# Grouped attention on one core: two heads' queries turned together, keys in both partition halves, scores of two heads in a row

## What is computed

```
A_HEADS = 8; A_KV_HEADS = 2; A_HEAD_DIM = 64
qa_l = apply_rope(qa_l, cos, sin)
ka_l = apply_rope(ka_l, cos, sin)
o_a = attend_blocks(qa_l, jnp.concatenate([ka_c, ka_l], axis=1), jnp.concatenate([va_c, va_l], axis=1))
# attend_blocks, for each block of 128 queries and each head h with keys of head h // 4:
#   p = softmax(q @ k.T * 64 ** -0.5);  o = p @ v
```

## Time and profile before

| | us |
|---|---|
| median of 3 runs | 1925.68 |
| lowest and highest | 1921.84, 1927.43 |
| the profiled execution | 1927.77 |
| its span from first to last instruction | 1925.9 |

### The profile page before, as it was taken

One profiled execution on the slowest core, in us unless ns is written; L12 is line 12 of the kernel. 1 busy time (PEld: TensorE's weight loads), 2 busy tenths in 40 slices (PEclk: granted clock), 3 DMA queues, 4 the chain that ended last, 5 costly groups with the idle time before them and its releaser, 6 DMA issues.

```text
span 1925.9 us, 22240 instructions
## 1 busy us (share of the span) xinstructions
PE 1629.5 (85%) x9130; PEld 1050.3 (55%) x9130; DVE 635.8 (33%) x1474; ACT 407.7 (21%) x725; POOL 41.5 (2%) x58
## 2 busy tenths in 40 slices
PE   6999999989999999998797776777787976776776
PEld 4544567878888886556543433433355542442433
DVE  3277453138898445548300000000023100000001
ACT  4221331011220113212321211111123211111211
POOL 0000000001210000001000000000000000000000
PEclk8999999999999989889798988888897998888888
DMA  9536740273749824103999999999986999999996
GB/s 366 180 111 221 284 156 1 88 284 132 261 150 375 316 80 175 44 1 138 427 414 430 428 428 429 428 428 428 417 338 246 430 428 429 428 428 428 428 428 259
DMA packets 110831, 572.56 MB, mean 297 GB/s; under 512 B 9188, under 2 KB 15460, under 8 KB 86184
## 3 DMA queue, kind: packets, MB, share of 16 engines
q1 hardware_dynamic: 109776, 569.79, 73.3%
q10 hardware_dynamic: 984, 1.79, 0.3%
HBM read 570.51 MB, written 1.05 MB: 297 GB/s over the span
## 4 chain that ended last, share of the span: by engine, by line
PE 60%; DMA 31%; DVE 4%; ACT 2%; issue 1%; SPq 1%; DVEq 0%; ACTq 0%
DMA ring<-in_w_exp_up_dram 30%; PE bank L483 19%; PE bank L1213 10%; PE bank L886 8%; PE bank L913 4%; PE bank L491 2%; PE bank L1239 2%; PE bank L929 2%; PE bank L1249 2%; PE bank L1289 1%; PE bank L570 1%; PE bank L1200 1%; DMA ring<-in_w_ada_dram 1%; PE bank L580 1%; PE bank L625 1%
## 5 line engine op out<-in xcount | busy, mean ns | idle before, releaser
L1213 PE MATMUL bank<-ring,arena 128*32 128x512 f32 x1792 | 267.8, 753 | 195.4 <-DMA ring<-in_w_exp_up_dram 193.4
L1213 PEld LDWEIGHTS bank<-ring,arena 128*32 128x32 f32 x1792 | 70.7, 134 | 389.8 <-issue 354.2
L2556 DVE COPY arena<-bank 128x256 f32<-128x256 f32 x32 | 13.6, 424 | 606.4 <-PE bank L1229 606.4
L886 PE MATMUL bank<-hT,ring 128*128 128x256 f32 x704 | 155.6, 383 | 4.2 <-ACT hT L1447 4.2
L483 PE MATMUL bank<-ring,hT 128*128 128x512 f32 (+3 forms) x416 | 148.5, 513 | 1.6 <-DVE arena L2343 1.5
L886 PEld LDWEIGHTS bank<-hT,ring 128*128 128x128 f32 x704 | 134.9, 192 | 23.1 <-issue 4.6
L1780 ACT COPY arena<-bank 128x512 f32<-128x512 f32 x32 | 33.4, 1044 | 440.6 <-PE bank L1213 440.6
L1239 PE MATMUL bank<-ring,arena 128*32 128x512 f32 x960 | 125.1, 666 | 1.7 <-DVE arena L2560 1.7
L1249 PE MATMUL bank<-arena 128*128 128x256 f32 x512 | 118.8, 385 | 1.8 <-DVE arena L2568 1.8
L1852 DVE SCALAR_TENSOR_TENSOR spare<-ring,spare 128x512 f32<-128x512 f32 x154 | 116.3, 755 | 4.4
L1249 PEld LDWEIGHTS bank<-arena 128*128 128x128 f32 x512 | 94.6, 190 | 39.7 <-issue 28.1
(11 more groups left out here) (358 smaller groups left out, 1702.8 us busy)
## 6 DMA issues: line engine op xcount, KB each, us to landing
ring<-in_w_exp_down_dram SPq DMA_DIRECT2D x60, 2048.0 KB, 19.1
ring<-in_w_exp_gate_dram SPq DMA_DIRECT2D x56, 2048.0 KB, 19.0
ring<-in_w_exp_up_dram SPq DMA_DIRECT2D x56, 2048.0 KB, 23.3
ring<-in_w_mod_dram SPq DMA_DIRECT2D x24, 2048.0 KB, 12.4
ring<-in_w_ada_dram SPq DMA_DIRECT2D x12, 2048.0 KB, 13.9
ring<-in_w_up_dram SPq DMA_DIRECT2D x10, 2048.0 KB, 11.2
ring<-in_w_in_dram SPq DMA_DIRECT2D x8, 2048.0 KB, 14.3
arena<-in_w_exp_up_dram SPq DMA_DIRECT2D x6, 2048.0 KB, 24.2
```

What stands on the lines that cost most here:

```text
L886: ins = pe.matmul(b[:, 0:T], x[:, k, j * 128:j * 128 + 128], hT[:, k, 0:T], start=(k == 0), stop=(k == KD - 1))
L1213: ins = pe.matmul(bank[0][32 * q:32 * q + 32, :], xe[:, k * CAP:(k + 1) * CAP], xs[q // 2][:, o:o + 512], start=(k == 0), stop=(k == KD - ...
```

## The change

Keys and queries are laid out anew. The keys of each key-value head are turned twice, once into partitions 0 to 63 and once into 64 to 127, by plain matmuls against the identity (16 matmuls of 64 by 128). The queries of two heads are turned together, 128 channels at a time (8 turns). Each engine now copies two banks of 128 partitions, where it copied three of 64. The order of the steps becomes pair of heads, block, head (`head_block`), so that two steps next to each other are the two heads of a pair: one reads partitions 0 to 63 of `e_qT` and `e_kT`, the other 64 to 127. PE issues the scores two at a time, at even i. The output of a pair of heads takes its bank from the first ring. The latent attention (`mla`) keeps its order.

```
+def head_block(tag, i):
+    pair, r = divmod(i, 4)
+    return (pair, r % 2, r // 2) if tag == "gqa" else (pair, r // 2, r % 2)
...
-        e_qT = ar(4096, A_H, T)
+        e_qT = ar(4096, A_H // 2, T)
...
                 def scores(i):
                     b = G.open(pe, (tag, "s", i), second=True)
-                    h, qb = i // 2, i % 2
+                    hp, h2, qb = head_block(tag, i)
+                    h = 2 * hp + h2
...
                 def output(hp):
-                    b = G.open(pe, (tag, "o", hp), second=True)
+                    b = G.open(pe, (tag, "o", hp), second=tag == "mla")
...
                 for i in range(2 * heads):
-                    if i + 2 < 2 * heads:
+                    if tag == "gqa" and i % 2 == 0 and i + 2 < 2 * heads:
+                        scores(i + 2)
+                        scores(i + 3)
+                    if tag == "mla" and i + 2 < 2 * heads:
                         scores(i + 2)
...
             for g in range(A_KV):
                 b = G.open(pe, ("ekT", g))
-                turn(("ekT", g), b, [e_kv[:, tb, g * A_D:g * A_D + A_D] for tb in range(4)])
+                for tb in range(4):
+                    for lo in (0, A_D):
+                        ins = pe.matmul(b[lo:lo + A_D, tb * 128:tb * 128 + 128], e_kv[:, tb, g * A_D:g * A_D + A_D],
+                                        ident, start=True, stop=True, skip_group_check=True)
+                G.close(ins, ("ekT", g))
             pe.wait_ge(sem("heads_ready"), 3)
-            for hp in range(4):
-                b = G.open(pe, ("eqT", hp))
-                turn(("eqT", hp), b, [e_qa[:, tb, h * A_D:h * A_D + A_D] for h in (2 * hp, 2 * hp + 1) for tb in range(TB)])
+            for half in range(2):
+                b = G.open(pe, ("eqT", half))
+                turn(("eqT", half), b, [e_qa[:, tb, hp * 128:hp * 128 + 128] for hp in (2 * half, 2 * half + 1)
+                                        for tb in range(TB)])
...
-            attend("gqa", A_H, lambda h: e_qT[0:A_D, h, :], lambda h: e_kT[0:A_D, h // 4, :],
+            attend("gqa", A_H, lambda h: e_qT[A_D * (h % 2):A_D * (h % 2) + A_D, h // 2, :],
+                   lambda h: e_kT[A_D * (h % 2):A_D * (h % 2) + A_D, h // 4, :],
...
-            G.give(act.copy(e_kT[0:A_D, 1, :], G.take(act, ("ekT", 1))[0:A_D, :]), ("ekT", 1))
-            for hp in (1, 3):
-                G.give(act.copy(e_qT[0:A_D, 2 * hp:2 * hp + 2, :].rearrange("p a b -> p (a b)"),
-                                G.take(act, ("eqT", hp))[0:A_D, :]), ("eqT", hp))
+            evict(("ekT", 1), e_kT[:, 1, :])
+            evict(("eqT", 1), e_qT[:, 2:4, :].rearrange("p a b -> p (a b)"))
...
-            G.give(dve.tensor_copy(e_kT[0:A_D, 0, :], G.take(dve, ("ekT", 0))[0:A_D, :]), ("ekT", 0))
-            for hp in (0, 2):
-                G.give(dve.tensor_copy(e_qT[0:A_D, 2 * hp:2 * hp + 2, :].rearrange("p a b -> p (a b)"),
-                                       G.take(dve, ("eqT", hp))[0:A_D, :]), ("eqT", hp))
+            evict(("ekT", 0), e_kT[:, 0, :])
+            evict(("eqT", 0), e_qT[:, 0:2, :].rearrange("p a b -> p (a b)"))
```

More of the change, by code:

```diff
@@ L965, in _ @@
                 b = G.open(pe, ("ekT", g))
-                turn(("ekT", g), b, [e_kv[:, tb, g * A_D:g * A_D + A_D] for tb in range(4)])
+                for tb in range(4):
[3 more added lines that the diff above has]
+                G.close(ins, ("ekT", g))
             pe.wait_ge(sem("heads_ready"), 3)
-            for hp in range(4):
-                b = G.open(pe, ("eqT", hp))
-                turn(("eqT", hp), b, [e_qa[:, tb, h * A_D:h * A_D + A_D] for h in (2 * hp, 2 * hp + 1) for tb in range(TB)])
+            for half in range(2):
+                b = G.open(pe, ("eqT", half))
+                turn(("eqT", half), b, [e_qa[:, tb, hp * 128:hp * 128 + 128] for hp in (2 * half, 2 * half + 1)
+                                        for tb in range(TB)])
             for g in range(A_KV):
                 G.read(pe, ("ekT", g))
-            for hp in range(4):
-                G.read(pe, ("eqT", hp))
+            for half in range(2):
+                G.read(pe, ("eqT", half))
             def gqa_fill(i):
@@ L1523, in transposed @@
             def transposed(eng, tag, i, prT):
-                h, qb = i // 2, i % 2
+                hp, h2, qb = head_block(tag, i)
                 b = G.take(eng, (tag, "pt", i))
-                if h >= 2:
-                    eng.wait_ge(done, G.number[(tag, "o", h // 2 - 1)])
-                to = prT[:, h % 2, :].rearrange("p (j t) -> p j t", j=4)[:, :, qb * 128:qb * 128 + 128]
+                if hp:
+                    eng.wait_ge(done, G.number[(tag, "o", hp - 1)])
+                to = prT[:, h2, :].rearrange("p (j t) -> p j t", j=4)[:, :, qb * 128:qb * 128 + 128]
                 src = b.rearrange("p (j t) -> p j t", j=4)
@@ L1970, in transposed @@
             def transposed(tag, i, prT):
-                h, qb = i // 2, i % 2
+                hp, h2, qb = head_block(tag, i)
                 b = G.take(dve, (tag, "pt", i))
-                if h >= 2:
-                    dve.wait_ge(done, G.number[(tag, "o", h // 2 - 1)])
-                to = prT[:, h % 2, :].rearrange("p (j t) -> p j t", j=4)[:, :, qb * 128:qb * 128 + 128]
+                if hp:
+                    dve.wait_ge(done, G.number[(tag, "o", hp - 1)])
+                to = prT[:, h2, :].rearrange("p (j t) -> p j t", j=4)[:, :, qb * 128:qb * 128 + 128]
                 G.give(dve.tensor_copy(to, b.rearrange("p (j t) -> p j t", j=4)), (tag, "pt", i))
```

## The result

| | before | after |
|---|---|---|
| median, us | 1926.44 (1921.84 to 1927.43, 4 runs) | 1915.29 (1913.66 to 1917.06, 4 runs) |
| profiled execution, us | 1927.77 | 1914.73 |
| its span, us | 1925.9 | 1912.9 |

The changed kernel takes 0.9947 of the time, with a 95% interval of 0.9928 to 0.9966: 10 to 11 us less. The forecast was 1921.2 with a range of 1916.5 to 1927.0.

What follows compares the result with a forecast made beforehand. PE's work in the attention was taken to set the start of the DMA-bound expert weight stream, and so the end. Gains of 2.01 + 3.15 less 0.66 make 4.5 us: 1925.7 - 4.5 = 1921.2, range 1916.5 to 1927.

Steps and rivals of the forecast that it cites:

- lost in the DMA stream: Rival: some expert weight load is not tied to PE, so the gain is lost; 1925.7 us, 5%.
- Turns, copies, bank rings: Ahead of the scores and at the outputs' banks: turns 2.85 us against 2.78, copies and banks without new waits; 0 each.
- First steps: Start of the attention: pt(0) stays at 763.64, earlier scores meet an idle PE, pt(1) follows VectorE; gain 0.
- The second score: Pairs at even steps: the second score in the other row half costs 0.11 us, six pairs 0.66.
- records that overlap by one only: Rival: a pair of scores takes three records' time instead of two; 2.2 us gained, 1923.5, 7%.
- The row halves don't overlap: Rival: a pair of scores costs 1.9 us at full clock; 0.8 us slower, 1926.5, 8%.
- What falls away: Odd steps lose their score: 2.01 us at step 3, 3.15 at 5, 7 and 9, less 0.66: 4.5 gained.
- The softmax: Middle of the attention: PE stays the bound by 0.25 us ahead of pt(6); rival that VectorE binds: 1924.3, 5%.
- The clock: PE's half clock early in the attention returns equally long after the first fill's start: 0, with 1.7 us each way.
- The forecast's own sign of being wrong: Expert load issue moves but the end doesn't, or the low clock after 764 lasts another length than 13.5 us.
- the clock comes back sooner: Rival: full clock is back by 771, so the first fill takes 3.7 us, not 6.1; 1918.8, 12%.
- The rivals of a longer low clock: Half clock lasts a stretch more (about 1924, 8%) or through the attention (22 us dearer, 1943, 6%).

Runs made afterwards that it cites:

- e1_apart: The changed kernel with scores issued one in every step again, new layout and order of steps kept: 1926.1 us, ratio 1.0 to before.
- e2_same_half: The changed kernel with the old layout, both scores of a pair in partitions 0 to 63, still issued two at a time: 1927.86 us, ratio 1.0001 to before.
- split: The changed kernel with three of four fills cut in halves at steps 1 and 3, 5 and 7, 9 and 11, the fourth whole at 13: 1911.38 us.
- full_rows: The kernel before with scores of 128 rows, partitions 64 to 127 of queries and keys set to zero: 1913.21 us, ratio 0.9937 to before.
- refill: The changed kernel with the four whole fills at steps 1, 5, 11 and 13 instead of 3, 5, 7 and 9: 1918.73 us, ratio 0.996 to before.
- full_warm: The kernel before with zero-padded scores of 128 rows, plus matmuls on constants in PE's idle time in the attention: 1911.28 us, ratio 0.992 to before.

## Why the prediction was right and wrong

- **What bounds the kernel: right.** In all kernels the first expert load moved with PE, and the end with it (1012.7 us from the one to the other after, 1013.3 before, 1011.8 to 1013.3 in all traces). The rival "lost in the DMA stream" falls.
- **Turns, copies, bank rings: right, with one price that was bounded well.** The 16 key matmuls take 1.90 us (752.72 to 754.62), taken as 1.95; the time from the first turn to the first score is 0.23 us longer, forecast as 0. e1_apart, which has all of this and nothing else, takes the time of before.
- **First steps: nearly right.** `pt(0)` ran wholly at half clock (1.05 instead of 0.74), which costs 0.3. The idle time ahead of `pt(1)` grew from 0.25 us to 2.25, forecast as 2.3 more.
- **The second score: right kind, too dear.** 0.11 was taken from L725; a pair costs 1.06 and one score 1.05, so 0.01. e2_same_half shows that it is the overlap of the two halves (1.91 without it). The rival of "records that overlap by one only" would have made a pair of about 1.5; it falls. The forecast drew it from the Trainium skill ("TensorE: Matmul & The Clock Gate", Part 3, The mechanism), by which matmuls keep program order in start and end. That rule itself isn't refuted: the pair's four records start at 772.68, 772.69, 773.21 and 773.22 us, by twos, so it holds if both scores' first records come ahead of both second ones; which record belongs to which score the trace doesn't say. "The row halves don't overlap" falls too.
- **What falls away: 4.5 forecast, 4.9 measured at full clock, with errors that cancel.** The 4.5 held 2.01 for step 3 at half clock. At full clock the forecast's own terms give 4 x 1.05 - 6 x 0.11 = 3.5. Measured is 4.9: each of the four odd steps brings 1.24 to 1.28 instead of 1.05 (turn and fill each take 0.1 less without a score of 64 rows between them), 0.8 more in all, and the six pairs cost 0.13 together instead of 0.66. Steps 11 and 13 brought nothing by this, as forecast. That 4.5 and 4.9 lie so close is luck: the one holds a part of the clock (2.01 - 1.05 = 0.96) that the other doesn't.
- **The softmax: PE and VectorE tie.** The margin ahead of `pt(6)` was forecast as 0.25 us. VectorE's scaling of step 6, in order of time after:

```profile
780.58 0.49 DVE L2006 TENSOR_SCALAR arena<-arena,small 128x512 f32<-128x512 f32 x1
```

  It ends at 781.07, PE follows 0.14 later, at 781.21, and the pair ahead of it takes 1.11 (780.10 to 781.21) where one ahead of an output takes 1.06. So the margin is gone: PE came 0.2 us sooner, by the fill (0.1) and the pair (0.1), VectorE 0.1 later than forecast (4.96 us behind the end of `pt(4)`, at 776.11, and not 4.86), and PE waits 0.05. The rival would have needed a microsecond. The Trainium skill ("TensorEngine Tiling (Array Packing)", PSUM Bottleneck) says that the emptying of PSUM may become the bottleneck once tiling has sped up TensorE. The traces agree at steps 11 and 13, where PE idles 2.25 us for the engines that read the scores and the turned probabilities, and by 0.05 us at step 6; split, with half a fill at step 5, waits 1.00 there.
- **The clock: the step that failed.** "I take 0, with 1.7 us each way." Beyond the 0.96 that step 3's score brought at half clock, the forecast had nothing for the clock, and the clock brought 4.9 us in all: 4.0 of the 5.3 us between the 4.5 forecast and the 9.8 of the attention are this term, and 1.35 are the work above. The working assumed that the clock comes back equally long after the fill's start, 4.9 us. It came back 0.2 us ahead of the fill in after (0.3 in the second trace). So the fill ran at full clock from its first record, 2.54 us shorter than before instead of nothing, and step 12's score and output, at half clock before, ran at full clock too (1.62 us less from `pt(11)` to `pt(13)`). The first steps took back 0.3. The forecast's own sign of being wrong was met: the low clock after 764 lasted 6.8 us and not 13.5. The rival "the clock comes back sooner" had the direction, 12% and 2.4 us; it priced the fill alone and left out the tail. The rivals of a longer low clock fall.

**What brought the clock back.** The low stretch that begins at `pt(0)` was 13.6 us long in before and in e1_apart, 10.2 in e2_same_half, 6.8 in after and 3.4 in full_rows. Counted from the start of the first fill, the clock returned 4.9 us later in before, 4.3 later in e1_apart, 1.8 later in e2_same_half, 0.2 ahead in after and 2.3 ahead in full_rows. e1_apart has the idle time, turns and copies of after, but single scores; so it isn't the layout or the new order of heads. e2_same_half has after's instructions in after's order, without the overlap. Its low stretch is 3.4 us shorter than before's, and 3.4 longer than after's: half of the shortening comes with the moving of the scores, and half with the use of both row halves. In after and full_rows the clock was back ahead of the fill, so it isn't the earlier fill that brings it.

One reading fits all five: what holds the clock down is the time that PE spends on matmuls of 64 rows alone. Between `pt(0)` and the first fill that is three single scores in before and e1_apart (6.2 us), two in e2_same_half (3.8), and none in after, where the pair uses both halves, and in full_rows. refill and split, which put fill matmuls of 128 rows right behind `pt(0)`, have a stretch of 3.4 us as well. The changes between 64 and 128 rows alone don't explain it, as e2_same_half and after have the same number of them; that they take part isn't excluded, since full_rows removes them too. No kernel here kept the changes and filled the rows with single scores, and all but before and after have one trace. So the reading is argued and not shown. Shown is the order of the lengths at this place, and that no low stretch began where PE's wait was filled with matmuls of 128 rows.

## What to carry to other kernels

Price a stretch at the clock that it will have after the change, not before it: a clock that falls in a short wait for the softmax can double the cost of all that follows, and here this was half of the gain. Read the granted clock in windows of both kernels ahead of any sum, and if an engine-bound stretch runs at half clock behind a wait, first fill the wait with matmuls on constants; that alone gave 13 us of 1926 in the old kernel, and together with the change and the filled waits of the mLSTM 23. Two matmuls of 64 rows in the two row halves cost one (1.06 us against 1.05), and what then bounds the loop in part of its steps is the chain over VectorE. Moving whole fills into those waits only moved the waits; cutting them in halves gave 0.6 us at full clock, and 2 more by the clock.

## What was not expected of the hardware

- **Fewer rows, more time.** A score of 64 rows and 512 columns takes 1.05 us between 128-row neighbours, one of 128 rows 0.86. The turns ahead take 0.59 and 0.49 (behind an output), the fills behind 3.56 and 3.46. Three scores in a row take 2.81 us with 64 rows and 2.81 with 128 (full_warm), so the surcharge is at the change and not in the matmul. The Trainium skill ("TensorEngine Tiling (Array Packing)", Tiling Modes, Key Properties) says that a change of tiling mode drains the engine; the rows agree with it, as the runs show a surcharge at the change, and give its size: 0.39 us for a lone score between a turn and a fill, so about 0.2 for each of the two changes. That it is a drain they don't show.
- **Filling half of the rows with zeros makes the kernel faster.** full_rows takes 1913.2 us against 1926, in the attention by 3.0 us of those changes and 6.7 of the clock.
- **The same wait, with and without a fall of the clock.** The wait of 2.25 us ahead of `pt(11)` in after left the clock at 1.00; the same wait ahead of `pt(3)` in refill was followed by half clock. The clock also stayed at 1.00 behind refill's own wait ahead of `pt(9)`, and in split from 766.2 to 807.2, through waits of 0.5 to 1.0 us in seven steps. What decides is not shown. In the attention the course repeated between two executions of the same kernel, shifted by up to 1 us; in the first 50 us it didn't.
